# A decoder step with a product-key expert layer: 192 tokens instead of 160 on fetched expert rows, 352 instead of 384 dense

## The reference

```
q      = (x @ w_q).reshape(8 heads, 2, 128)
s1, s2 = q[:, 0] @ sub_keys[0].T, q[:, 1] @ sub_keys[1].T     # 128 scores each
v1, i1 = top_k(s1, 16);  v2, i2 = top_k(s2, 16)
sv, si = top_k(v1[:, None] + v2[None, :], 16)                 # 16 of 256 pairs
e      = i1[si // 16] * 128 + i2[si % 16]                     # 128 picks a token
gate   = softmax(sv)
act    = gelu(peer_u[e] . x)
out    = sum(gate * act * peer_v[e])
```

## Time and profile before

| | before |
|---|---|
| median of 3 runs | 4757.61 us (4756.5 to 4760.84) |
| profiled execution, its own time | 4756.15 us |
| span of that execution | 4754.1 us |
| PE busy | 4350.0 us, 91% |
| DVE busy | 2941.9 us, 62% |
| ACT, POOL busy | 1155.8 us, 1134.0 us |
| bytes moved | 923.58 MB |
| mean granted clock of PE | 0.926 |

### The profile page before, as it was taken

One profiled execution on the slowest core, in us unless ns is written; L12 is line 12 of the kernel. 1 busy time (PEld: TensorE's weight loads), 2 busy tenths in 40 slices (PEclk: granted clock), 3 DMA queues, 4 the chain that ended last, 5 costly groups with the idle time before them and its releaser, 6 DMA issues. The chain is left out here.

```text
span 4754.1 us, 69606 instructions
## 1 busy us (share of the span) xinstructions
PE 4350.0 (91%) x28073; PEld 4008.7 (84%) x28073; DVE 2941.9 (62%) x4239; ACT 1155.8 (24%) x1507; POOL 1134.0 (24%) x695
## 2 busy tenths in 40 slices
PE   5997898898898967996999999999998999999997
PEld 4776777777677756895999999999997999999996
DVE  1243244443443443334996778777877988889886
ACT  0132211112112211213222332333222222222223
POOL 0000012112112111003345333333331333333330
PEclk6998988888888867997999999999998999999998
DMA  8221222222122112412234899999997888888884
GB/s 332 87 82 57 74 70 73 71 70 82 62 70 82 43 52 73 159 62 81 82 113 147 326 336 341 331 341 333 333 344 287 335 327 341 325 327 332 335 299 159
DMA packets 208669, 923.58 MB, mean 194 GB/s; under 512 B 20961, under 2 KB 105057, under 8 KB 109153
## 3 DMA queue, kind: packets, MB, share of 16 engines
q1 hardware_dynamic: 91104, 526.16, 29.8%
q0 software_dynamic: 49408, 344.48, 19.6%
q10 hardware_dynamic: 67968, 50.34, 3.2%
HBM read 854.62 MB, written 66.28 MB: 194 GB/s over the span
## 5 line engine op out<-in xcount | busy, mean ns | idle before, releaser
L92 PE MATMUL PS<-first_HH,tail_WH 128*128 128x384 f32 (+1 forms) x3072 | 1004.7, 327 | 41.9 <-DVE first_HL L1487 32.0
L93 PE MATMUL PS<-first_HL,tail_WH 128*128 128x384 f32 (+1 forms) x3072 | 987.7, 322 | 0.0
L94 PE MATMUL PS<-first_HH,tail_WL 128*128 128x384 f32 (+1 forms) x3072 | 985.5, 321 | 0.0
L92 PE MATMUL PS<-dn_BH,tail_WH 128*128 128x384 f32 x2048 | 687.5, 336 | 23.0 <-DVE dn_BL L2001 22.5
L94 PE MATMUL PS<-dn_BH,tail_WL 128*128 128x384 f32 x2048 | 686.1, 335 | 0.0
L93 PE MATMUL PS<-dn_BL,tail_WH 128*128 128x384 f32 x2048 | 686.1, 335 | 0.0
L92 PEld LDWEIGHTS PS<-first_HH,tail_WH 128*128 128x128 f32 x3072 | 580.7, 189 | 44.1 <-issue 38.2
L93 PEld LDWEIGHTS PS<-first_HL,tail_WH 128*128 128x128 f32 x3072 | 580.7, 189 | 0.5
L94 PEld LDWEIGHTS PS<-first_HH,tail_WL 128*128 128x128 f32 x3072 | 579.5, 189 | 0.0
L1974 POOL DMA_INDIRECT dn_VR<-in_v_rows,tail_EI x160 | 341.4, 2134 | 753.4 <-DVEq L2020 718.1
L1758 POOL DMA_INDIRECT up_UR<-in_u_rows,tail_EI x160 | 344.2, 2151 | 613.6 <-DVEq L1852 586.5
(11 more groups left out here) (366 smaller groups left out, 6204.9 us busy)
## 6 DMA issues: line engine op xcount, KB each, us to landing
tail_WR<-in_peer_u SPq DMA_DIRECT2D x128, 1024.0 KB, 6.8
tail_WR<-in_peer_v SPq DMA_DIRECT2D x128, 1024.0 KB, 5.9
mix_RING<-in_w_ada SPq DMA_DIRECT2D x96, 1024.0 KB, 4.9
mix_RING<-in_w_in SPq DMA_DIRECT2D x42, 1024.0 KB, 4.9
tmp_z<-up_ZB ACTq DMA_DIRECT2D x128, 192.0 KB, 4.3
tmp_gd<-up_STG ACTq DMA_DIRECT2D x24, 1024.0 KB, 16.7
dn_GG<-tmp_gd SPq DMA_DIRECT2D x16, 1536.0 KB, 8.9
dn_ZI<-tmp_z SPq DMA_DIRECT2D x128, 192.0 KB, 3.7
```

The lines of the kernel that those rows point to most:

```text
L92: nc.tensor.matmul(out, r32(wh), r32(xh), start=first, stop=False)
L93: nc.tensor.matmul(out, r32(wh), r32(xl), start=False, stop=False)
L94: return nc.tensor.matmul(out, r32(wl), r32(xh), start=False, stop=last)
```

## The change

`TD` falls from 384 to 352, so 352 tokens are dense and 192 fetched: 128 on a partition each (352 to 479), and a second group of 64, the last 32 prompt tokens and the 32 sample tokens, on two partitions each (`REP` = 2). The second group now takes 64 gathers in place of 32, `PICKS` is 192, and there are 88 gate groups. Every matmul of the up and down tiles has 352 columns. ACT copies a query tile in four pieces, where there were three. The final phase folds two partitions instead of four, over two banks, and applies the prompt's gate to 32 of the 64 columns.

```diff
--- before.py
+++ after.py
@@ -40,8 +40,9 @@
 HEADS, TOPK = 8, 16
 JG = 8
 NG = NK // JG
-TD = 384
-NR4 = NB * NS
+TD = 352
+NR4 = T - TD - P
+T4 = TD + P
 REP = P // NR4
 PICKS = P + P // REP
 PARTS = ((0, TH), (TH, T))
@@ -1427,9 +1428,9 @@
             for kt in range(KT):
                 pe.wait_ge(h2_ready, kt + 1)
                 at = slice(P * (kt % 4), P * (kt % 4) + P)
-                nc.tensor.transpose(PS[:, kt // 4, at], TMP[:, kt % 4, TD:SEQ], IDENT[:])
+                nc.tensor.transpose(PS[:, kt // 4, at], TMP[:, kt % 4, TD:T4], IDENT[:])
                 for r in range(REP):
-                    mm = nc.tensor.matmul(PS[NR4 * r:NR4 * r + NR4, 4 + kt // 4, at], TMP[:, kt % 4, SEQ:T], IDENT[:],
+                    mm = nc.tensor.matmul(PS[NR4 * r:NR4 * r + NR4, 4 + kt // 4, at], TMP[:, kt % 4, T4:T], IDENT[:],
                                           start=True, stop=True)
                 mm.then_inc(xs_done, 1)
 
@@ -1551,7 +1552,7 @@
     PS, IDENT, XS, XR, CF, EI = (g[x] for x in ("PS", "IDENT", "XS", "XR", "CF", "EI"))
     WR, WH, WL, HH, HL = (g[x] for x in ("WR", "WH", "WL", "HH", "HL"))
     ZB = m.sb("ZB", [P, 2, TD])
-    RT = m.sb("RT", [P, 3, TD])
+    RT = m.sb("RT", [P, 3, 3 * P])
     EG = m.sb("EG", [P, NT, 3, P])
     ZS = m.sb("ZS", [P, PICKS])
     IOTA = m.sb("IOTA", [P, NK])
@@ -1656,7 +1657,7 @@
                     u_tile(n % 2, lo_pool, 8 * it + (NQ + n + 1), 8 * it + (NQ + n + 1))
             pe.wait_ge(eg_ready, 1)
             pe.wait_ge(sc_ready, NQ + 1)
-            for t in range(TD // P):
+            for t in range(3):
                 for j in range(3):
                     mm = nc.tensor.transpose(PS[:, 4 + t, P * j:P * j + P], EG[:, t, j, :], IDENT[:])
                 mm.then_inc(rt_ready, 1)
@@ -1706,9 +1707,10 @@
             for i in range(NQ):
                 act.wait_ge(used, i + 1)
                 A(QT[:, i % 2, 0:TH], PS[:, 2 * (i % 2), 0:TH], ACT.Copy)
-                A(QT[:, i % 2, TH:SEQ], PS[:, 2 * (i % 2) + 1, 0:SEQ - TH], ACT.Copy)
-                A(QT[:, i % 2, SEQ:SEQ + P].rearrange("p (r t) -> p r t", r=REP),
-                  bcast(PS[:, 2 * (i % 2) + 1, SEQ - TH:TH], 1, REP), ACT.Copy).then_inc(q_ready, 1)
+                A(QT[:, i % 2, TH:3 * P], PS[:, 2 * (i % 2) + 1, 0:3 * P - TH], ACT.Copy)
+                A(QT[:, i % 2, 3 * P:4 * P], PS[:, 2 * (i % 2) + 1, TD - TH:T4 - TH], ACT.Copy)
+                A(QT[:, i % 2, 4 * P:5 * P].rearrange("p (r t) -> p r t", r=REP),
+                  bcast(PS[:, 2 * (i % 2) + 1, T4 - TH:TH], 1, REP), ACT.Copy).then_inc(q_ready, 1)
                 act.drain().then_inc(bank_free, 1)
                 high(i + 2)
                 if i:
@@ -1854,7 +1856,7 @@
             for n in range(UA, NK):
                 low(NQ + n)
                 if n == UA:
-                    dve.wait_ge(rt_read, TD // P)
+                    dve.wait_ge(rt_read, 3)
                 for b in batches_of(n):
                     one_hot(b)
                 for j in dots_of(n):
@@ -2058,8 +2060,8 @@
         def _(pe):
             pe.wait_ge(sum4_ready, 1)
             for kt in range(KT):
-                mm = nc.tensor.matmul(PS[:, 4, NR4 * kt:NR4 * kt + NR4], YR[:, P * kt:P * kt + P], SUM4[:],
-                                      start=True, stop=True)
+                mm = nc.tensor.matmul(PS[:, 4 + kt // 8, NR4 * (kt % 8):NR4 * (kt % 8) + NR4], YR[:, P * kt:P * kt + P],
+                                      SUM4[:], start=True, stop=True)
             mm.then_inc(ss_done, 1)
             for kt in range(KT):
                 nc.tensor.transpose(PS[:, kt // 4, P * (kt % 4):P * (kt % 4) + P], YS[:, P * kt:P * kt + P],
@@ -2073,7 +2075,7 @@
         @block.scalar
         def _(act):
             act.wait_ge(ss_done, 1)
-            nc.scalar.activation(SS[:], PS[:, 4, :].rearrange("p (k t) -> p k t", k=KT), ACT.Copy).then_inc(ss_read, 1)
+            nc.scalar.activation(SS[:].rearrange("p (h k) t -> p h (k t)", h=2), PS[:, 4:6, :], ACT.Copy).then_inc(ss_read, 1)
             for q in range(4):
                 act.wait_ge(x_in[q], 16)
                 nc.scalar.activation(XT[:, 4 * q:4 * q + 4, :], XT[:, 4 * q:4 * q + 4, :], ACT.Copy,
@@ -2089,19 +2091,21 @@
             dve.drain().then_inc(sum4_ready, 1)
             norm.start(dve)
             dve.wait_ge(ss_read, 1)
-            ss = SS[:].rearrange("p k (b s) -> p k b s", s=NS)
+            sp = SS[:, :, 0:SEQ - T4]
+            V.tensor_tensor(sp, sp, bcast(MOD[:, 5 * KT:6 * KT, 0], 2, SEQ - T4), ALU.mult)
+            ss = SS[:, :, SEQ - T4:NR4].rearrange("p k (b s) -> p k b s", s=NS)
             V.tensor_tensor(ss, ss, bcast(MOD[:, 5 * KT:6 * KT, 1:9], 3, NS), ALU.mult)
             dve.drain()
             for kt in range(KT):
                 gate = MOD[:, 5 * KT + kt, 0:1]
                 if kt % 4 == 0:
                     dve.wait_ge(x_scaled, kt // 4 + 1)
-                    xs = XT[:, kt:kt + 4, SEQ:T]
+                    xs = XT[:, kt:kt + 4, T4:T]
                     V.tensor_tensor(xs, xs, SS[:, kt:kt + 4], ALU.add)
                 V.scalar_tensor_tensor(XT[:, kt, 0:TD], YA[:, kt, :], gate, XT[:, kt, 0:TD], ALU.mult, ALU.add)
                 dve.wait_ge(ys_done, 4 * (kt // 4) + 4)
-                V.scalar_tensor_tensor(XT[:, kt, TD:SEQ], PS[:, kt // 4, P * (kt % 4):P * (kt % 4) + P], gate,
-                                       XT[:, kt, TD:SEQ], ALU.mult, ALU.add).then_inc(x_ready, 1)
+                V.scalar_tensor_tensor(XT[:, kt, TD:T4], PS[:, kt // 4, P * (kt % 4):P * (kt % 4) + P], gate,
+                                       XT[:, kt, TD:T4], ALU.mult, ALU.add).then_inc(x_ready, 1)
             dve.drain()
             norm.vector(dve)
```

## The result

The changed kernel takes 4723.29 us (median of 5 runs, 4705.46 to 4735.03) against 4756.5 for the kernel before: a ratio of 0.993 with an interval of 0.9911 to 0.9949, a gain of 33 us. The profiled execution took 4705.46, the fastest of the five, 18 us under their median; over the five executions the time goes with PE's mean granted clock, from 0.923 in this one to 0.916 in the slowest.

| us | up to first copy | first 24 | late up | down | behind |
|---|---|---|---|---|---|
| before | 2432.0 | 193.9 | 963.2 | 1095.8 | 69.2 |
| after | 2422.0 | 178.6 | 937.3 | 1092.8 | 73.2 |
| difference | -10.0 | -15.3 | -25.9 | -3.0 | +4.0 |
| predicted | 0 | -15.5 | -11 | -20 | +1.5 |

The account below looks back on a forecast made before the run. PE bounds every tile before; afterwards transfers were to bound late up and DVE down. -15.5 (first 24 tiles) - 11 (late up) - 20 (down) + 1.5 (rest) = -45 us, giving 4712 us, range 4665 to 4785.

Parts of the forecast that it names:

- Columns: Dense matmuls: 32 columns less at 0.43 ns each, 0.66 us a tile; spacing at 352 columns near 160 ns.
- the first 24 tiles: Start of the up stage: tiles of 7.77 us, PE still last, gain 24 x 0.66, written as -15.5 us.
- Late up: Last 104 up tiles: transfers become the bound, 352 MB at 370 GB/s, 952 us, -11 us.
- PE's floor: Late up: least time of PE, 88 tiles with a gate table and 16 without, 886 us.
- The end at 397 GB/s: Late up: if the engines reach this rate, PE's floor of 886 us holds, -77 us.
- the slower rival at 350: Late up and down: mixed traffic sustains only 350 GB/s, +43 us and +25 us, 4812 in all; chance 0.25.
- Down: 128 down tiles: DVE becomes the bound at 8.06 us, 8.16 with waits, against 8.32 before; -20 us.
- The step that failed: Out stage: half of PE's repeated copies go, PE waits for DVE there, so 0 us.
- the prediction's own signs of being wrong: Late up following PE at 8.7 us a tile; a down tile below 8.06 or above 8.32; clock leaving 1.00.
- The clock: Down: DVE as bound opens gaps in PE and the clock falls, +64 us, 4776 in all; chance 0.07.
- The rest: Final stage: larger copy, wider matmuls and one more gate product, +1.5 us, 0 to 5.
- The sum: All terms: -15.5 - 11 - 20 + 1.5 = -45 us, giving 4712 us.

Follow-up runs that it names:

- half_dma: `pad` with gathers fetching 4 KB instead of 8 KB a partition, the other half of the buffers cleared beforehand: 4610.11 us, ratio 0.9702.
- pad: Changed kernel with 28 repeated copy matmuls in the out stage, so PE's program before the down loop is as long as before: 4677.38 us, ratio 0.9834.
- dense_only: `pad` without the second group's 32 additional picks, so half of that group's rows are left out: 4563.45 us, ratio 0.9591.
- half_dve: `pad` with each row product taking 1024 of the 2048 columns, all transfers kept: 4618.17 us, ratio 0.972.
- before_shift: Kernel before with 36 more repeated matmuls in the out stage, moving PE's down loop to its place in the changed kernel: 4809.51 us, ratio 1.011.
- zsp: Changed kernel with the z stores issued by SP between weight loads instead of by ACT: 4713.63 us, ratio 0.9917.
- rest_pool: Changed kernel with the edits of `pad` and `zsp`, and 120 of 128 low parts of gate products moved from DVE to POOL: 4676.37 us, ratio 0.983.

## Why the prediction was right, and where it was wrong

- *Columns and the first 24 tiles.* The spacing of 159.6 ns and -15.3 us agree with both steps (24 x 0.66 is 15.8, not the 15.5 written).
- *Late up.* The mechanism held: transfers took PE's place, and `half_dma` shows it. The size was off: 370 GB/s was taken from the stage's own traffic, 375 to 378 were sustained. The term of -11 measured -26 in the changed kernel and -19 in `pad`, whose up stage is the same. PE's floor was sized ten us too high [`dense_only`]. The end at 397 GB/s was not reached, nor the slower rival at 350.
- *Down.* DVE as the bound was right, and `half_dve` shows it; the tile was sized 0.10 too long, 8.16 where `pad` has 8.06 in all. Worked out as in the prediction, DVE's own part in `pad` is 7.98 (940 us less 9.2 of idle time before low parts and rows, in 116.6 tiles) against 8.06, and 0.08 is idle against the 0.10 that was left for waits. That 8.06 stands in both sums is chance. Without the stops the term is -36, not -20.
- *The step that failed* is the one costed at nothing: "The out stage drops half of the repeated copies on PE, which waits for DVE there: 0." The dropped copies do cost nothing where they stood. But they moved PE's down loop to a place where it is fetched in each pass: 1092.8 us in down against 1059.6 in `pad`, 33 us in the profiles and 46 between the medians. Down's -20 became -3. No row of before shows this; the only sign in its trace is the count of 130 packets. Two of the prediction's own signs of being wrong came with it: a down tile over 8.32 (8.37), and a clock that left 1.00.
- *The clock.* The rival had the price of gaps right in kind, but from the wrong gaps: DVE's short ones leave the clock at 1.00 in `pad`'s down stage, and where the loop stops it is 0.98 (changed kernel) and 0.97 (`before_shift`). In late up, where PE waits 37.8 us in all for DVE's low parts, it is 0.99.
- *The rest.* The stretch behind the last matmul grew by 4.0 us, not 1.5. The fold took 7.10 and its copy 1.02, against 7.05 and 0.60:

```profile
4634.60 7.10 PE PS L2063 x32
...
4641.72 1.02 ACT fin_SS L2078
```

  Of the 4.0 us, 0.4 are this copy; 1.5 are a longer wait of DVE for PE between the two stages (2.97 us, before 1.52), and 1.5 a group of LayerNorm matmuls at a clock of 0.89 (15.59 us, before 14.06 at 1.00). With the same final stage, `dense_only` and `half_dve` have 68.7 to 68.9, with the wait at 1.52 and the matmuls at 14.06 to 14.07. Where the longer wait comes from stays open.
- *The sum* was right partly by luck: in the profiled executions late up gave 15 us more than predicted and the untouched stages 10, down 17 less. Without the step that failed, the gain is 78 us [`pad`], not the 45 forecast.

## What to carry to other kernels

An edit of an engine's program moves a loop that stands behind it, and here, on PE, that alone changed its time. Compare the count of instruction packets and the "issue" waits of before and after first: the stops that they show cost 46 of 78 us, and 28 repeated matmuls gave them back. When one resource is relieved, price the next two by the time of the first that still covers them: the same 32 gathers cost 3 us under a long cover and 114 under a shorter one.

## What the runs showed of the hardware

- A PE loop of 16 tiles is kept or fetched again according to the number of instructions ahead of it: 130 against 193 packets of 16 KB, two stops of 1.6 to 4.3 us a pass, and the 1.2 GHz level for 3.4 to 10.2 us of each pass.
- A store can hold the engine that issues it: the issue of a z store on ACT took 8.36 us in late up (0.33 is the median), and the copy of the gate table behind it waited 6.54:

```profile
2754.48 8.36 ACTq L1727 DMA_DIRECT2D tmp_z<-up_ZB  x1
...
2762.94 0.60 ACT L1698 ACTIVATE up_STG<-PS 128x512 f32<-128x512 f32 x1 [6.54 <-issue]
```

  In the changed kernel 14 of the 22 z stores that come next behind a gate store on ACT took over 1 us to issue, and 2 of the 22 after those; none of the other 84 did, and none on SP in `zsp`. Why a gate store ahead has this effect was not tested.
- One core sustained 382 GB/s over 850 us of mixed loads, gathers and stores (`half_dve`), above the 370 that the busy share had suggested.
- POOL and DVE hold each other up, one of the two at a time (`rest_pool`): 62 POOL operations that began during a row product took 0.96 us and the row product 3.18; the 58 that began during a low part on DVE took 2.23 and the low part its usual 2.29.
